# Gate and up weights side by side in one moving operand of 512 columns, and stage changes by row blocks

## What is computed

```
def swiglu(h, w_gate, w_up, w_down):
    return (jax.nn.silu(h @ w_gate) * (h @ w_up)) @ w_down

x = x + m @ w_out                                  # block one; then h = rms_norm(x, norm2_g)
x = x + swiglu(h, w_gate, w_up, w_down)
# block two, twice (fox, S5):
h = rmsnorm(x, mix_pre_gain[i]);  m = mixer(h)
x = x + rmsnorm(m, mix_post_gain[i])
h = rmsnorm(x, ffn_pre_gain[i])
x = x + rmsnorm(swiglu(h, ...), ffn_post_gain[i])
```

## Time and profile before

| | us |
|---|---|
| runs | 1005.13, 1005.32, 1005.66 |
| profiled execution, span from first to last instruction | 1002.9 |
| time outside the span (median less span) | 2.4 |
| PE busy | 974.8 (97%) |
| DVE busy | 616.3 (61%) |
| ACT busy | 492.4 (49%) |
| POOL busy | 316.2 (32%) |

### The profile page before, as it was taken

How to read it: one execution, slowest core, us unless ns; L and a number is a source line. 1 busy time by engine, 2 the same in 40 slices (tenths; PEclk the granted TensorE clock), 3 DMA queues, 4 the chain that set the end, 5 groups by cost and what they waited for, 6 DMA issues and landing times.

```text
span 1002.9 us, 17059 instructions
## 1 busy us (share of the span) xinstructions
PE 974.8 (97%) x6948; PEld 874.4 (87%) x6948; DVE 616.3 (61%) x648; ACT 492.4 (49%) x659; POOL 316.2 (32%) x331
## 2 busy tenths in 40 slices
PE   8999899999999999999999999999989999999997
PEld 6987679999988778788889999887969889999886
DVE  4899766666664555465665555535686665655544
ACT  6765564444433466545564434433566464344332
POOL 5670457799899217761020000001100020000000
PEclk9999999999999999999999999999999999999999
DMA  9742046777666845545555655556963646556551
GB/s 337 267 135 75 1 153 212 229 220 222 221 226 225 251 154 176 168 130 171 159 170 175 198 172 179 199 185 230 389 226 130 204 132 196 179 167 207 170 168 42
DMA packets 131138, 186.79 MB, mean 186 GB/s; under 512 B 4752, under 2 KB 103568, under 8 KB 130576
## 3 DMA queue, kind: packets, MB, share of 16 engines
q1 hardware_dynamic: 106944, 158.28, 48.4%
q10 hardware_dynamic: 24144, 27.81, 8.2%
HBM read 174.54 MB, written 15.73 MB: 190 GB/s over the span
## 4 chain that ended last, share of the span: by engine, by line
PE 86%; DVE 7%; ACT 3%; issue 2%; POOL 2%; ACTq 0%; DVEq 0%; POOLq 0%
PE ps L419 15%; PE ps L421 14%; PE ps L420 14%; PE ps L473 7%; PE ps L477 7%; PE ps L475 7%; PE ps L440 4%; PE ps L442 4%; PE ps L441 4%; DVE cacc L2147 2%; ACT whi L373 1%; PE ps L901 1%; DVE wlo L379 1%; PE ps L920 1%; PE ps L1004 1%
## 5 line engine op out<-in xcount | busy, mean ns | idle before, releaser
L379 DVE TENSOR_TENSOR wlo<-wraw,whi 128x2048 fp32r<-128x2048 f32 x141 | 335.3, 2378 | 229.7 <-ACT whi L373 229.3
L373 ACT ACTIVATE whi<-wraw 128x2048 fp32r<-128x2048 f32 x143 | 273.6, 1914 | 362.2 <-PE ps L421 218.0
L419 PE MATMUL ps<-actH,whi 128*128 128x256 f32 x1232 | 351.7, 285 | 1.4 <-DVE actL L606 1.1
L420 PE MATMUL ps<-actL,whi 128*128 128x256 f32 x1232 | 348.5, 283 | 0.0
L421 PE MATMUL ps<-actH,wlo 128*128 128x256 f32 x1200 | 339.5, 283 | 0.0
L419 PEld LDWEIGHTS ps<-actH,whi 128*128 128x128 f32 x1232 | 236.3, 192 | 5.2 <-issue 3.9
L420 PEld LDWEIGHTS ps<-actL,whi 128*128 128x128 f32 x1232 | 236.4, 192 | 0.1
L421 PEld LDWEIGHTS ps<-actH,wlo 128*128 128x128 f32 x1200 | 230.2, 192 | 0.0
L654 POOL TENSOR_SCALAR ss<-ss 128x1 f32<-128x1 f32 x8 | 2.3, 285 | 455.1 <-ACT sg L627 454.8
L473 PE MATMUL ps<-whi,gH 128*128 128x512 f32 x256 | 79.6, 392 | 0.0
L477 PE MATMUL ps<-whi,gL 128*128 128x512 f32 x256 | 78.9, 389 | 0.0
(11 more groups left out here) (388 smaller groups left out, 1355.8 us busy)
## 6 DMA issues: line engine op xcount, KB each, us to landing
wraw<-in_ffn_w_gate SPq DMA_DIRECT2D x22, 1024.0 KB, 5.5
wraw<-in_ffn_w_up SPq DMA_DIRECT2D x22, 1024.0 KB, 5.5
wraw<-in_ffn_w_down SPq DMA_DIRECT2D x22, 1024.0 KB, 5.0
wraw<-in_fox_w_in SPq DMA_DIRECT2D x16, 1024.0 KB, 5.4
wraw<-in_w_gate SPq DMA_DIRECT2D x11, 1024.0 KB, 5.4
wraw<-in_w_up SPq DMA_DIRECT2D x11, 1024.0 KB, 5.7
wraw<-in_w_down SPq DMA_DIRECT2D x11, 1024.0 KB, 5.1
wraw<-in_w_in SPq DMA_DIRECT2D x9, 1024.0 KB, 11.5
```

What stands on the lines that cost most here:

```text
L373: act.activation(self.high_of(n0), self.wraw[:, n0 % RAW, :], ACT.Copy).then_inc(self.hi_done, 1)
L379: dve.tensor_tensor(self.low_of(n0), self.wraw[:, n0 % RAW, :], self.high_of(n0).bitcast(F32), ALU.subtract).then_inc(self.lo_done, 1)
L419: pe.matmul(out, wh, self.actH[:, k, :], start=(i == 0), stop=False)
L420: pe.matmul(out, wh, self.actL[:, k, :], start=False, stop=False)
```

## The change

1. **Pairs.** A unit of f.up now holds 512 rows of K with 256 gate and 256 up columns side by side (two transfers of 512 KB). `mm_quarter` holds activations still and moves 512 weight columns: 48 matmuls of 512 columns a pair, tokens on partitions. Silu takes 1/rms as a scale for each partition straight from PSUM, two of 128x256, and DVE's product is 128x512. The product is turned back to features on partitions by four PE transposes (`pe_gated_turn`, L821), which stand after the sixth of the next pair's eight quarters (that of the last pair inside the second down unit). gH and gL read PSUM. `pe_spread`, `rdiag` and L745 go from f1, f2 and f3.
2. **Stage changes by row blocks.** The last unit of o1, f1 and f3 and the last two of o2, o3 and f2 finish row block 0 first (`mm_last_rows`). x of a row block is turned in two groups of four 128x128 pieces. The first pair is done for row block 0, then for row block 1 (`mm_first_rows`), with the transposes of row block 1 between.
3. **Early buffers.** High parts of first units of f1, fox, f2, s and f3 and of some last units go to buffers of their own (`early_*`), and the low part is written over the raw unit, so these splits don't wait for the ring. The raw buffer of such a unit is loaded again only when PE has used it.
4. **Around fox.** 24 small matmuls for forget gates (`forget_logits`) move from between fox's first two units into row block 1's second unit. Two transfers of post-norm gains move from ahead of fp to behind the first `block_out` of fox. The units are numbered from `first["fox"]` as fox+0, fox+1 and so on.
5. **Post-norm.** In `dve_postnorm` row block 0's two additions to x now stand before `norm(2)`. Before S5, `act_spread` moves ahead of a table's transfer.

The core of the diff:

```diff
-    def pe_pair(self, pe, st, n0, a, f0, it=0, f_step=0, ready=None, late=None):
...
-        self.mm_features(pe, n0, a, it, ready, late=late)
...
-        self.mm_features(pe, n0 + 1, a + 1, it, middle=None if f0 > 0 else lambda: self.pe_spread(pe, st, 0))
+    def pe_pair(self, pe, st, n0, f0, it=0, f_step=0):
...
+        if f0 >= 2:
+            pe.wait_ge(*self.past(st + "_prod", f - 1))
+        for h in range(2):
+            for k in range(4):
+                if (h, k) == (1, 2):
+                    self.pe_gated_turn(pe, st, f0 - 1, it, f_step)
+                self.mm_quarter(pe, n0 + h, banks, h, k, it=it)
+    def act_pair(self, act, st, n0, f0, it=0, f_step=0):
...
+        self.split_high(act, n0 + 2, it)
         if f0 > 0:
+            self.act_gated_high(act, st, f0 - 1, it, f_step)
+        self.split_high(act, n0 + 3, it)
...
+            act.activation(self.sg[:, 256 * r:256 * r + 256], self.ps[:, banks[r], 0:256], ACT.Silu,
+                           scale=self.rx[:, r:r + 1]).then_inc(self.sem(st + "_silu"), 1)
+    def mm_first_rows(self, pe, st, n0, banks, second_row, between=None):
+        for r in range(RT):
+            for h in range(2):
+                pe.wait_ge(self.lo_done, n0 + h + 1)
+                for k in range(4):
+                    if (r, h, k) == (0, 1, 2):
+                        second_row(0)
...
+                    pe.wait_ge(*self.past(st + "_act_ready", KT * r + 4 * h + k + 1))
+                    self.mm_quarter(pe, n0 + h, banks, h, k, low=(self.lo_done, n0 + h + 1), rows=(r,))
+            if r == 0:
+                second_row(1)
...
+                if i == 0:
+                    for t, name in enumerate(("mix_post_gain_2", "ffn_post_gain_2")):
+                        act.dma_start(m.gb[t][:], io[name][0:1, :].to_broadcast([P, D]))\
```

## The result

The changed kernel is slower: 1015.21 us (1011.02 to 1016.19) against 1005.23, a ratio of 1.0089 with an interval of 1.0072 to 1.0106. I had forecast 999.6, and 1006 as the upper end.

What follows compares the result with a forecast made beforehand. PE, busy 97% of the span, was taken as the bound. Terms -5.7 + 1.35 + 0.1 + 3.5 - 3.6 - 1.7 + 0.3 = -5.75 gave 999.6 us; own range 996 to 1002.5, 8-in-10 range 992 to 1006.

Steps and rivals of the forecast that it cites:

- The pairs: Pairs 2 to 11 of f1, f2, f3: -0.64 for matmuls, +0.45 for transposes, net -0.19 each, -5.7 in all.
- turned product: Rival, in pairs: four transposes cost 0.64, so pairs are worth nothing; 1005.9 us, chance 0.15.
- 512 columns cost two of 256: Rival, in pairs: fewer matmuls save nothing, a pair takes 0.45 more than before; 1018.8 us, chance 0.03.
- the second unit late: Rival, in every pair: second unit's split exceeds its 1.0 us margin; 1008.6 us if 1.3 late, chance 0.11.
- o2 to f2: Last o2 matmul to f2's second pair: 17.1 us becomes 15.3, -1.8, held by a late split; f3 alike.
- o1 to f1: Last o1 matmul to f1's second pair: 16.3 us becomes 16.4, +0.1; second low split some 1.1 us late.
- f1 to fox: Two new PE waits, 2.6 to 3 in f1's last down unit and 3.4 before fox+3; +3.5 for fox+4.
- Could a transfer be later still? ... This costs nothing: Start of f2: second pair's units, loaded later into o2's raw buffers, still land in time, at no cost.
- -5.75: Whole kernel: sum of all forecast terms, taking the profiled span from 1002.9 to 997.2 us.
- the slower ones: Rivals in pairs: second unit's split late (1008.6 us, 0.11); 512-column matmuls costing two of 256 (1018.8 us, 0.03).

Runs made afterwards that it cites:

- split_before_squares: Changed kernel with ACT's copy of the second pair's first unit ahead of the two squares in f2 and f3: 1008.33 us, ratio 1.0025.
- fox_split_first: Changed kernel with ACT's copy of fox+1 ahead of the last S5 table group, two gain transfers behind fox+3's copy: 1008.84 us, ratio 1.0034.
- s5_table_first: Changed kernel with OTab's 4 MB transfer issued ahead of act_spread before S5 again: 1015.78 us, ratio 1.0096.
- s0_low_apart: Changed kernel with the low part of s's first unit in its own buffer instead of over the raw unit: 1013.73 us, ratio 1.0083.
- f2_one_unit: Changed kernel with f2 ending by row blocks over one unit, s's second split, OTab's transfer and act_spread ordered as before: 1015.86 us, ratio 1.0086.
- after_fills: Changed kernel with 30 filling matmuls on PE ahead of each of five new waits (f1, fp first transposes; second pairs of f1, f2, f3): 1009.16 us, ratio 1.0038.
- the second profile of before: The kernel before, unchanged, measured and profiled once more for its granted clock: 1005.42 us.

## Why the prediction was wrong

**The pairs were right.** In f2, from the second product on:

```profile
L875 DVE TENSOR_TENSOR prod<-sg,ps x10: 680/680/684, 547.3 to 649.5; 128x512 f32<-128x512 f32 x10
```

That is 11.36 a pair, 11.33 forecast, with no PE wait inside. The four transposes in it:

```profile
539.65 0.60 PE L821 MATMUL ps<-ident,prod 128*128 128x128 f32 x4
540.00 0.48 PE L469 MATMUL ps<-whi,actH 128*128 128x512 f32 x1
540.32 0.40 PE L470 MATMUL ps<-wlo,actH 128*128 128x512 f32 x1
```

They took 0.35 to the next matmul, which itself started the following one after 0.32 instead of 0.23: 0.45 in all, as forecast. So neither the "turned product" nor the "512 columns cost two of 256" came about, and "the second unit late" did not either. In f1 a pair took 12.40, not 12.32, and in three of the ten the table groups came late: 1.9 us in all, 1.25 of it with the wait for POOL that begins at 208.4. From the second pair to the first down unit it took 125.86 us (159.48 to 285.34) instead of 125.07 (155.26 to 280.33): f1's ten pairs lost 0.8 where I had a gain of 1.9.

**"o2 to f2" and f3: right but for the clock.** The waits behind the first pair were 2.3 and 2.6; I had 2.5. From the end of o2's last matmul to the second pair it took 14.8 us (514.96 to 529.71), 15.3 forecast. `split_before_squares` shows that the cause is one of those named, the squares ahead of the copy: without them f2's wait goes and 0.5 of f3's is left.

**"o1 to f1": the wait at the first transposes was mis-sized,** 2.2 instead of 1.1. The two low splits of the changed kernel took not the 2.29 of the earlier trace rows, where POOL had nothing to do (DVE, then POOL):

```profile
134.19 3.13 DVE L409 TENSOR_TENSOR wrawlow<-wraw,early_gain 128x2048 fp32r<-128x2048 f32 x1 [0.45 <-ACT early_gain L403]
137.25 3.14 DVE L409 TENSOR_TENSOR wrawlow<-wraw,early_nat 128x2048 fp32r<-128x2048 f32 x1
...
134.12 1.06 POOL L961 TENSOR_TENSOR rtb<-G,Bri 128x512 f32<-128x512 f32 x1
135.14 3.10 POOL L961 TENSOR_TENSOR otmp<-G,Bri 128x512 f32<-128x512 f32 x1
138.32 3.21 POOL L970 TENSOR_TENSOR rtb<-rtb,otmp 128x512 f32<-128x512 f32 x1
```

POOL was busy for 5.92 of the 6 us from 134 on. The Trainium skill ("SBUF — State Buffer", section "SBUF: two separate sides") lets a DVE operation with two operands in SBUF and a POOL operation that reads SBUF exclude each other for whole instructions; the trace agrees, 0.85 us for each split, and POOL's operations of 135.14 and 138.32 grew likewise: the same two took 1.06 and 1.30 in the kernel before, where they began ahead of DVE's split. That split took 2.71, beside POOL's next operation, so a row nearer than the earlier trace rows stood in the trace. Wherever POOL was idle beside it in the changed kernel's profile, a split took 2.27 to 2.32. No run took POOL's work away at this place, so the cause is read from the trace and not shown by an experiment.

**"f1 to fox": first wait right (2.55 against 2.6 to 3), second half of it.** Before fox+3 PE waited 1.7, not 3.4. The two gain issues lay beside ACT's table load (at 371.9 and 372.3) and `ka` followed directly, so the 1.06 for them was not to be paid; `fox_split_first` shows the same from the other side.

**The term that was missing: S5, +6.2.** The step that failed is "Could a transfer be later still? ... This costs nothing". I asked it of the start of f2 (and, alike, f3) alone, and the sum has no term for S5. Each early unit keeps its raw buffer until PE has used it, and at f2's end two of the four were kept, so glu's two units went out behind RTab and in front of OTab and shared the memory with 8 MB. The Trainium skill ("DMA: Bandwidth & Descriptors", section "Queues, rings and completion order") says that the transfer engines take packets of the queues in turn, by which a unit on one queue slows down beside a table on another; the trace agrees, with 23.0 us to landing for glu's second unit where a unit alone took some 5. `s5_table_first` and `s0_low_apart` show that neither the table's place nor one of the buffers alone is the cause, `f2_one_unit` that giving both buffers back ends it. (That run also has the split of s's second unit and OTab's transfer back in their old places; the latter, alone, had not helped.)

**The other one: the granted clock, 5 to 6.** The earlier trace rows show PE at full clock, and I priced every row at it. I counted the new waits, but not the matmuls behind them at 1.2 GHz. The trace of before had such a place as well, behind PE's wait of 2.1 us ahead of s; in a slice of the page it does not show:

```profile
700.00:704.00 4.00, 4.00 (x30) 3.56 (x28) 2.87 (x6) 0.97 (x3) 0.74 (x1) 0.58 1.11 431
```

`after_fills` measures the three new places together: 6.0 us by the medians, 5.1 by the two ratios (1.0089 less 1.0038), with the waits in place. With S5's 6.2 (low clock in and behind its wait included, which the fills left as it was) that is 11.3 to 12.2. My -5.75 with f1's pairs (2.7) and its first wait (1.1) put right is -1.95, and together they make 9.4 to 10.3 of the 10.0. Two smaller terms nearly cancel: fox's second wait was 1.7 shorter than I had it, and 1.1 of the first stretch's 4.9 is not the change's, since the second profile of before has it too. One sum of mine was wrong beside this: the bounds that I named for my own range add up to 994.7 to 1001.6, not 996 to 1002.5. The measured time lies outside either.

No rival had either of the two: the slower ones looked for a loss that repeats in every pair, while the losses came once each, at stage changes.

## What to carry to other kernels

A wait that is added to the engine that is the bound costs its own length and, where the clock falls behind it, some 2 us more here (5 to 6 us over three waits of 2.2 to 2.6): price it with the matmuls that follow, or fill it. When a buffer is held longer, follow its queue to the next two or three transfers and to what else moves at that time, in every stage, not only in the one that gained. A split or a copy that becomes ready early is worth what stands ahead of it in its engine's order; put first what the bound engine needs first.

## What was unexpected of the hardware

A spell at half clock in the attention (0.50 at 108 to 112 us) cost only about 1 us, since PE would have waited next for DVE anyway. Waits of 2.2 to 2.6 us without fills were followed by a lower clock in six of eight profiles at f1, five of six at fp, five of six at f2 and four of six at f3 (in neither of the two of the changed kernel), the instructions being the same; what decides it was not settled.
